# Branch products of the gated merges formed from seven quarter products

## What is computed

```python
# first block: two branches, o_a and o_b are [512, 512], w_proj_* are [512, 1024]
gates = jax.nn.sigmoid(gate_logits.reshape(b, s, N_BRANCHES, d) + b_gate)
merged = gates[:, :, 0] * (o_a @ w_proj_a) + gates[:, :, 1] * (o_b @ w_proj_b)
x = x + (merged @ w_out).astype(x.dtype)
# second block, twice: three branches, each ys[:, :, n] is [512, 512], w_branch[l][n] is [512, 1024]
br = jnp.einsum('bsnc,ncd->bsnd', ys, w_branch[l])
gates = jax.nn.sigmoid(g_logits.reshape(B, S, N_BRANCH, D) + gate_b[l])
merged = jnp.sum(gates * br, axis=2)
x = x + rmsnorm_2(merged @ w_out[l], post_g[l])
```

## Time and profile before

| what | value |
|---|---|
| median of 3 runs | 3052.73 us (3052.6 to 3055.26) |
| the profiled execution: its own time | 3055.15 us |
| its span, first to last instruction | 3053.3 us |
| mean granted TensorE clock | 0.978 of 2.4 GHz |
| merge stage of the first block | 461.92 to 615.85 us of the span |
| merge stages of the layers | 2143.37 to 2348.79 us and 2784.98 to 2990.4 us |
| experts of the first block | about 720 to 1735 us |

### The profile page before, as it was taken

How to read it: one execution, slowest core, us unless ns; L and a number is a source line. 1 busy time by engine, 2 the same in 40 slices (tenths; PEclk the granted TensorE clock), 3 DMA queues, 4 the chain that set the end, 5 groups by cost and what they waited for, 6 DMA issues and landing times.

```text
span 3053.3 us, 42832 instructions
## 1 busy us (share of the span) xinstructions
PE 2843.7 (93%) x15470; PEld 1702.8 (56%) x15471; DVE 1200.2 (39%) x2569; ACT 802.6 (26%) x1607; POOL 115.4 (4%) x132
## 2 busy tenths in 40 slices
PE   7989889998999989998999689999999999999999
PEld 6874567754333333333333278585676595666774
DVE  6771674224222222222222265435333454444332
ACT  3221571111222222222222223414111224322111
POOL 0000100000000000000000000011000000110000
PEclk9999999997999999999999889999999999999999
DMA  4222002237999999999999742031221331112221
GB/s 176 83 70 69 15 1 97 83 112 299 421 418 423 405 420 404 405 407 414 403 411 407 308 149 87 28 107 35 90 83 57 102 102 52 66 63 76 83 69 69
DMA packets 119627, 578.08 MB, mean 189 GB/s; under 512 B 13933, under 2 KB 19437, under 8 KB 85712
## 3 DMA queue, kind: packets, MB, share of 16 engines
q1 hardware_dynamic: 110000, 559.37, 47.2%
q0 software_dynamic: 9504, 17.07, 1.5%
HBM read 572.97 MB, written 20.97 MB: 195 GB/s over the span
## 4 chain that ended last, share of the span: by engine, by line
PE 79%; DMA 11%; DVE 5%; ACT 2%; issue 2%; DVEq 1%; ACTq 0%; POOLq 0%; SPq 0%
PE banks L400 29%; PE banks L1593 11%; DMA arena<-in_w_up 10%; PE banks L337 8%; PE banks L1089 7%; PE banks L1634 5%; PE banks L842 4%; PE banks L820 3%; PE banks L1601 3%; PE banks L855 2%; PE banks L831 2%; PE banks L1640 2%; PE banks L276 1%; DVE arena L908 1%; PE banks L1573 1%
## 5 line engine op out<-in xcount | busy, mean ns | idle before, releaser
L400 PE MATMUL banks<-arena 128*128 128x256 f32 (+2 forms) x4256 | 917.5, 376 | 19.0 <-ACT arena L437 7.9
L400 PEld LDWEIGHTS banks<-arena 128*128 128x128 f32 x4256 | 797.3, 191 | 128.4 <-issue 21.9
L1593 PE MATMUL banks<-arena 128*64 128x512 f32 x2048 | 470.4, 606 | 54.4 <-DMA arena<-in_w_up 37.3
L1593 PEld LDWEIGHTS banks<-arena 128*64 128x64 f32 x2048 | 157.0, 138 | 322.8 <-issue 320.6
L437 ACT ACTIVATE arena<-banks 128x512 f32<-128x512 f32 (+2 forms) x152 | 89.1, 587 | 622.6 <-PE banks L400 622.6
L337 PE MATMUL banks<-arena 128*128 128x512 f32 x576 | 250.0, 592 | 0.0
L1634 PE MATMUL banks<-arena 128*64 128x512 f32 x1024 | 236.1, 599 | 0.0
L453 DVE TENSOR_TENSOR arena<-banks,arena 128x512 f32<-128x512 f32 (+2 forms) x114 | 77.4, 679 | 382.7 <-PE banks L400 381.2
L1089 PE MATMUL banks<-arena 128*128 128x512 f32 x512 | 222.9, 593 | 3.7 <-DVEq L206 3.7
L1735 DVE TENSOR_TENSOR arena<-banks,arena 128x512 f32<-128x512 f32 x64 | 44.3, 692 | 460.6 <-PE banks L1619 239.8
L385 DVE TENSOR_TENSOR arena<-arena 128x1024 f32<-128x1024 f32 (+2 forms) x152 | 182.6, 1201 | 21.2 <-issue 18.5
(11 more groups left out here) (242 smaller groups left out, 2398.6 us busy)
## 6 DMA issues: line engine op xcount, KB each, us to landing
arena<-in_w_up SPq DMA_DIRECT2D x128, 2048.0 KB, 24.4
arena<-in_w_down SPq DMA_DIRECT2D x128, 1024.0 KB, 22.0
arena<-in_w_in SPq DMA_DIRECT2D x76, 1024.0 KB, 5.0
arena<-in_w_out SPq DMA_DIRECT2D x12, 1024.0 KB, 5.1
arena<-in_w_branch SPq DMA_DIRECT2D x24, 512.0 KB, 4.6
arena<-expert_rows SPq DMA_DIRECT2D x4, 2048.0 KB, 14.7
arena<-in_w_in SPq DMA_DIRECT2D x2, 2048.0 KB, 10.0
arena<-in_w_in SPq DMA_DIRECT2D x4, 832.0 KB, 4.5
```

What stands on the lines that cost most here:

```text
L400: last = PE.matmul(PS[:, bank, t * width:(t + 1) * width], one[:, t * P:(t + 1) * P], other, start=(first and t == 0 and kk == 0), stop=(t ...
L1593: last = PE.matmul(PS[HB * s:HB * (s + 1), 4 + h], xT[:, k, 0:HB], gate_up(2 * h + s, k), start=(k == 0), stop=(k == 7))
```

## The change

The branch products become quarter products too. `Quarters` takes the left operand, the weights, the semaphores of their arrival and a distance `behind` as arguments, and its depth is 2 instead of 4 for a branch (inner dimension 512): each of the seven products is 2 x 2 multiplications of 128 rows by 256 columns, 56 instructions in a run. `gated` takes the place of `apply`. All branch products are changed but the first (n = 0, b = 0) of each layer, which stays plain (`whole_branch`). Runs of gates and branches alternate in `part_mm`. For each branch VectorE makes four sums (128x512) and four differences (128x512) at the head of its list for this (n, b), ScalarE four more copies. The order to the transfers is the same, but for w_out, whose first half now waits for product 0 of the last branch run and no more for product 0 of the last gate run, and whose second half waits for product 4 of the last branch run and no more for its end.

```diff
@@ -349,20 +349,24 @@
 
 
 
-            def __init__(self, sums, diffs, parts, made):
-                self.sums, self.diffs, self.parts, self.made = sums, diffs, parts, made
+            def __init__(self, sums, diffs, parts, made, still=None, weights=None, arrived=("w0_in", "w1_in"), behind=1):
+                self.sums, self.parts, self.made = sums, parts, made
+                self.diffs = diffs if isinstance(diffs, list) else [diffs + 1024 * i for i in range(4)]
+                self.still, self.weights, self.arrived, self.behind = hT if still is None else still, weights or Wh, arrived, behind
+                self.depth = self.weights[0].shape[1]
 
...
@@ -380,8 +384,8 @@
                 for i in some:
                     name, x, y, last_use = (("T1", "B12", "B11", 3), ("T2", "B22", "T1", 4),
                                             ("T3", "B22", "B12", 6), ("T4", "B21", "T2", 7))[i]
-                    dve.wait_ge(SEM["w0_in" if i == 0 else "w1_in"], 16 * L + 16)
-                    dve.wait_ge(SEM["part_mm"], up(7 * (F - 1) + last_use))
+                    dve.wait_ge(SEM[self.arrived[0 if i == 0 else 1]], 16 * L + 16)
+                    dve.wait_ge(SEM["part_mm"], up(7 * (F - self.behind) + last_use))
                     V.tensor_tensor(self.b(name, w), self.b(x, w), self.b(y, w), ALU.subtract).then_inc(SEM["mixed_w"], 1)
                     V.drain()
...
@@ -451,6 +455,25 @@
                 dve.wait_ge(SEM["part_out"], up(4 * F + put))
                 one = self.part(1, w) if bank is None else of(bank)
                 V.tensor_tensor(to, one, self.part((0, 2, 3, 3)[i], w), ALU.add).then_inc(SEM["ev"], 1)
+
+            def gated(self, dve, c, i, gates, merged, begun):
+
+                F = c.of("F")
+                row, col = ((0, 0), (0, 1), (1, 1), (1, 0))[i]
+                bank, after, put = ((1, 2, 1), (2, 5, 3), (None, 6, 4), (3, 7, 4))[i]
+                other, to = ((None, 0), (None, 2), (3, 1), (None, 3))[i]
+                g, m = (a[:, 2 * row:2 * row + 2, 256 * col:256 * col + 256] for a in (gates, merged))
+                dve.wait_ge(SEM["part_mm"], up(7 * F + after))
+                dve.wait_ge(SEM["part_out"], up(4 * F + put))
+                one = self.part(other, 256) if bank is None else PS[:, bank].rearrange("p (t x) -> p t x", t=2)
+                V.tensor_tensor(self.part(to, 256), one, self.part(to, 256), ALU.add)
+                V.drain()
+                V.tensor_tensor(g if begun else m, g, self.part(to, 256), ALU.mult).then_inc(SEM["ev"], 1)
+                if begun:
+                    V.drain()
+                    V.tensor_tensor(m, m, g, ALU.add)
+                if i % 2:
+                    V.drain().then_inc(SEM["applied"], 2)
 
         def unit(c, k, tt):
...
 
             merged = v2(base, TT, D)
             over = 1 if early else 0
-            KC = {"T": 2 * nbr - over, "M": nbr, "F": nbr - over, "L": nbr - over, "B": nbr, "sig": 4 * nbr}
+            all_gates = 2 * nbr - over
+
+            def at(c0, n, b, branch):
+
+                g = n * nbr + b - over
+                c = At(c0)
+                c["T"] = c0.of("T") + over + 2 * g + branch
+                c["F"] = c0.of("F") + 2 * g + branch
+                c["L"] = c0.of("B") + n * nbr + b if branch else c0.of("L") + g
+                c["sig"] = c0.of("sig") + 4 * (n * nbr + b)
+                return c
...
-                        if n or b > over:
-                            dense_sp(sp, c, b, gate_weights(c0, n, b), quartered=of_gates(n, b), done=-n * nbr)
-                        if n or b >= over:
-                            sp.wait_ge(SEM["mm"], up(4 * (c.of("M") + b)))
+                        g = n * nbr + b - over
+                        if g > 0:
+                            dense_sp(sp, c0, g, gate_weights(c0, n, b), quartered=2 * g - 1, done=0)
+                            sp.wait_ge(SEM["part_mm"], up(7 * (c0.of("F") + 2 * g)))
+                        elif g == 0:
+                            sp.wait_ge(SEM["mm"], up(4 * (c0.of("M") + over)))
+                        if g >= 0:
                             branch_weights(sp, c0, n, b)
...
                         if n or b >= over:
-                            Q(c).pe(pe, c, b + of_gates(n, b), of_gates(n, b), hooks=hooks)
-                        branch(pe, c, n, b)
+                            Q(c0).pe(pe, at(c0, n, b, 0), 0, 0, hooks=hooks)
+                            branch_of(c0, n, b).pe(pe, at(c0, n, b, 1), 0, 0)
+                        else:
+                            whole_branch(pe, c0)
...
-                        part(0)
-                        part(1)
+                        gates, branch = Q(c0), branch_of(c0, n, b)
+                        gates.act(act, c, 0, 0, 0)
+                        gates.act(act, c, 0, 0, 1)
                         back(0)
                         back(1)
-                        part(2)
+                        gates.act(act, c, 0, 0, 2)
                         back(2)
                         back(3)
                         sig(0)
                         sig(1)
-                        part(3)
+                        gates.act(act, c, 0, 0, 3)
+                        branch.act(act, cb, 0, 0, 0)
                         sig(2)
                         sig(3)
+                        branch.act(act, cb, 0, 0, 1)
+                        branch.act(act, cb, 0, 0, 2)
+                        branch.act(act, cb, 0, 0, 3)
...
+                        c, cb = at(c0, n, b, 0), at(c0, n, b, 1)
+                        gates, branch = Q(c0), branch_of(c0, n, b)
+                        if not n and b < over:
+                            for tt in range(TT):
+                                dve.wait_ge(SEM["sig_out"], up(c.of("sig") + tt + 1))
+                                dve.wait_ge(SEM["mm"], up(made(c0, 0, tt)))
+                                V.tensor_tensor(merged[:, tt, 0:512], v(early(tt), 512), PS[:, tt], ALU.mult).then_inc(SEM["ev"], 1)
+                                V.drain().then_inc(SEM["applied"], 1)
+                            continue
...
+                        branch.mix(dve, cb, 0, some=(0, 1))
+                        dve.wait_ge(SEM["part_mm"], up(7 * (cb.of("F") - 2) + 6))
+                        branch.sums_dve(dve)
+                        branch.mix(dve, cb, 0, some=(2, 3))
+                        for i in (0, 2):
+                            gates.dve(dve, c, 0, 0, i, v2(GS, TT, 512))
+                            gates.dve(dve, c, 0, 0, i + 1, v2(GS, TT, 512))
                             V.drain()
-                            logits(0)
-                            logits(1)
-                            result(2)
-                            result(3)
-                            V.drain()
-                            logits(2)
-                            logits(3)
-                            if n * nbr + b + 1 < 2 * nbr:
-                                Q(c).mix(dve, c, of_gates(n, b) + 1)
-                        for tt in range(TT):
-                            apply(tt)
...
+                            logits(i)
+                            logits(i + 1)
+                        if n * nbr + b + 1 < 2 * nbr:
+                            gates.mix(dve, at(c0, *divmod(n * nbr + b + 1, nbr), 0), 0)
+                        for i in range(4):
+                            if i % 2 == 0:
+                                dve.wait_ge(SEM["sig_out"], up(c.of("sig") + i + 2))
+                            branch.gated(dve, cb, i, v2(GS, TT, 512), merged[:, :, 512 * n:512 * n + 512], b > 0)
...
@@ -2291,7 +2329,9 @@
         merge_1, turn_last_1, mT, _ = merge_stage(
             BIG + 4096, BIG + 12288, BIG + 14336, 2, [v2(OA, 4, S), v2(OB, 4, S)], lambda c, b: A["w_proj_a"] if b == 0 else A["w_proj_b"],
             (lambda c: w_in, 5376), lambda c: A["b_gate"], BIG + 16384,
-            lambda c: Quarters([BIG + 18432, BIG + 19456, BIG + 20480, BIG + 25600], BIG, PARTS2, 1))
+            lambda c: Quarters([BIG + 18432, BIG + 19456, BIG + 20480, BIG + 25600], BIG, PARTS2, 1, behind=2),
+            lambda c, g, yT, w: Quarters([SC, SC + 512, SC + 1024, SC + 5120], [SC + 2048, SC + 2560, SC + 4096, SC + 4608], PARTS2, 2 + g,
+                                         yT, w, ("wb0_in", "wb1_in"), 2))
...
+            (w2, 4512), lambda c: A["gate_b_2"][bass.ds(c.of("layer"), 1)].rearrange("o w -> (o w)"), SC, q2_far,
+            lambda c, g, yT, w: Quarters([YA + 512 * i for i in range(4)], [LB + 10240 + 512 * i for i in range(4)], PARTS2,
+                                         7 + 6 * c.of("layer") + g, yT, w, ("wb0_in", "wb1_in"), 2), early_gate)
```

## The result

| | before | changed |
|---|---|---|
| median of the runs | 3053.99 us (4 runs) | 3033.41 us (3030.63 to 3040.78, 4 runs) |
| ratio | | 0.993, interval 0.9918 to 0.9942 |
| profiled execution, its time and span | 3055.15, 3053.3 us | 3040.78, 3039.0 us |

The medians differ by 20.6 us. The forecast was 3029.3 us, within 3024 to 3037. The same kernel timed twice more gave 0.9936 (0.9922 to 0.9949) and 0.9934 (0.992 to 0.9947). The mean of the three, 0.9933, is 20.4 us of 3054: faster by 0.7%, with every interval clear of 1, and 3 us less than the forecast's 23.4.

The account below looks back on a forecast made before the run. The prediction took PE's unbroken stream to bound the merges: 14 branch products at 1.67 us won each, other costs 0, give 23.4 us off 3052.73, so 3029.3 us; own range 3025 to 3034, with the absorbed case 3024 to 3037.

Parts of the forecast that it names:

- The price of a branch run: Merges: 56 instructions at the gate run's 0.2158 us, 12.09 instead of 13.76 us, 1.67 us won per branch product.
- The costs at nothing: Merges: VectorE's operands and gated quarters and ScalarE's copies stay under cover, costing PE 0 us.
- The gated product: VectorE behind a gate run ending at G: first multiplication ends at G + 8.9, PE wants it at G + 12.1.
- The copies: ScalarE in branch runs: 1.1 us of slack for products 4, 5 and the next gate's product 0, cost 0.
- The end of a merge and the transfers: Last branch: 0 cost with 1.1 us of slack, at most 1 us per stage; later first half of w_out costs 0.
- The sum: Whole kernel: 23.4 us less, 6.7 of it ahead of the experts and 16.7 behind; median 3029.3 us.
- the case in which this part is absorbed: Rival: transfers ahead of or in the experts arrive at the same absolute time, 6.7 us lost, 3036 us; chance 0.05.
- The signs of being wrong: L400 waiting for L437 or `gated` in merges, a 56-instruction run over 12.5 us, or longer stages behind the merges.
- Copies late: Rival in the merges: PE waits for ScalarE inside the short products, +12 us, 3065 us; chance 0.04.
- VectorE late: Rival in the merges: VectorE's list misses the 3.2 us slack, 1 us lost per pair, 3043 us; chance 0.04.
- Narrow dearer: Rival in branch runs: a 256-column instruction costs 0.23 us in short groups, 11 us lost, 3040 us; chance 0.03.
- No change: Rival: the branch product stays bound by something other than its columns, nothing gained; chance 0.02.

Follow-up runs that it names:

- the narrow kernel: Kernel before, each 512-column multiplication of the branch products made as two of 256, no sums or differences: merges 154.36 and 206.07 us, a single execution 3058.04 us.
- timed half-changes: Changed kernel with the old merge code in the layers, or in the first block: ratio to the kernel before 0.9989 (first block only changed) and 0.9944 (layers only changed).
- dve_plus4: Changed kernel, VectorE making the next gate run's first difference four extra times ahead of the gated quarters: merges 156.94, 214.42 and 211.02 us, single execution 3076.41 us.
- act_plus3: Changed kernel, ScalarE making each of the last three copies of a branch run four times instead of once: merges 160.49 and 213.77 us, single execution 3076.14 us.
- all_quarters: Changed kernel with each layer's first branch product made from quarter products too: layer 0's merge 197.43 us, ratio to the kernel before 0.9925.

## Why the prediction was right

**What bounds.** Right: in the merges PE is busy without a gap before and after, and the gain is in its stream.

**The price of a branch run.** 12.09 us forecast, 12.1 measured, and 23.0 us over the 14 against 23.4. The gate run's price per instruction was the right row; the narrow kernel confirms it apart from the seven-product scheme. VectorE's and ScalarE's additions were sized 2 us too high each (116 and 33 us against 113.7 and 31.1), which nothing hung on.

**The costs at nothing.** Each was given with its cover, and each cover was measured. The gated product was forecast at G + 8.9 and a slack of 3.2 us; it came at G + 9.1 with 3.1, and the kernels with extra work place the threshold at about 2.8 us of delay, where two of the three merges grow by 0.3 us; at 5.5 PE waits in every pair. The copies were forecast at 1.1 us of slack; they have it, and the threshold lies between 0.67 and 2.0 us. No run shows how much of the rest of the copies' slack is usable.

**The end of a merge and the transfers.** No wait appears at the head of the product with w_out in any of the three stages, and the first half of w_out, issued later than before, delays nothing.

**The sum.** Here the prediction was 3 us too good. It took for granted that what is won ahead of the experts stays won: "their stream moves with it", and gave the case in which this part is absorbed 0.05. The prediction looked for the absorption in the transfers. PE's mean idle time in the experts doesn't show it there (85.4 and 85.6 us). By the timed half-changes the first block's 6.6 us bring 3.4 (0.6 to 6.1). Full absorption, and full keeping by a hair, lie outside of that. One part is seen, a 3.4 us stretch at the low clock at the head of layer 0 in some executions; the other, in the experts' stage, is 1.8 us more of PE's busy time for the same instructions, a difference of means within the spread. Why the clock falls so stays open. The total still fell inside the forecast's own range, up to 3034 us, because that had room for dearer runs, for waits at three merge ends and for spread. The first two of these didn't occur. It is luck that the room left for them was enough for a loss of another kind.

**The signs of being wrong.** Most of what the prediction named is as it said: 4704 instructions of 256 columns, two plain products left (64 instructions of L1123), 9.7 us of idle time ahead of the quarter products, no wait for a copy or a gated quarter. One sign of being wrong did appear: the experts were longer than before, by 8.6 us in the profiled execution. The sign was drawn too tight, since the kernel before shows 3.5 us of it against itself.

**The rivals.** "Copies late" and "VectorE late" are real mechanisms whose point was not reached: forced, each puts a single execution 20 us above one of the kernel before (3076.14 and 3076.41 against 3056.24). The prediction had put the copies' case at 0.84 us for each handoff and 3065 us; the forced one, with a delay of 2.0 us, cost 1.1 us at each on average. "Narrow dearer" would have needed 0.014 us per instruction; it was 0.001. "No change" is out, since every interval lies below 1.

## What to carry to other kernels

When a tuned stage is bound by one engine without gaps, an edit that takes work from it is worth its own price in that stage, read from rows of the same form. How much of it reaches the total has to be timed. The other question is whether the helpers' additions stay under cover, and that is answered by walking one period with times, not by busy shares. A cover is a threshold, and past it the loss can exceed the wait itself: find the slack in the timeline, and test it with a dose below and one above. If the first of a series has less time than the others, give it an order of its own: for the first product here the differences of the next run belong behind the gated quarters.

## What the runs showed of the hardware

A pause of PE of 2.3 to 2.7 us, in a stage that otherwise streamed without a gap, was followed by 3.4 us at the 1.2 GHz level in seven of the eleven places in the three merges, and made a wait of 2.4 us cost up to 4.1 (dve_plus4). Pauses of 0.5 to 1.3 us, three to a branch run, never had that effect (act_plus3), nor had the one of 1.7 us in all_quarters. So in these kernels a stall ahead of a matrix product had two prices, and the larger one came only with the longer stalls.

The experts' stage, in which the transfers have a share of 0.98, differs by up to 9.5 us between executions of kernels that are the same in it (1006.1 to 1015.6 us). PE's busy time for its 6639 or 6640 instructions differs by 6.1 us (921.1 to 927.2), and its idle time by 8.0 (81.2 to 89.2). Changes of a few microseconds elsewhere are better read from their own stretch than from the total.
